# The last shared pass of a mixture-of-experts loop behind all passes of a single expert, its loads last in the queue

## The chip, the cores and the metric

The kernel runs on one core of one Trainium2 chip. The metric is the device time of one execution in microseconds (us), the median of three runs. Beside it stands one profiled execution, whose span is counted from its first to its last instruction; all rows below are from that execution.

## The reference, cut to what matters

The program is one decoder block on 256 tokens of width 1024: a convolution and an attention mixer first, then a mixture of 64 experts, of which each token takes 8. The change touches only the experts:

```
def expert_chunk(args):
    tc, cc = args                                   # 256 tokens, their weights for 64 experts
    gu = jnp.einsum('cd,edf->cef', tc, w_experts_gate_up)          # (64, 1024, 512)
    act = jax.nn.silu(gu[..., :EXPERT_DIM]) * gu[..., EXPERT_DIM:] * cc[..., None]
    return jnp.einsum('cef,efd->cd', act, w_experts_down)          # (64, 256, 1024)
...
x = x + gate2 * moe_sublayer(h, ...)      # routed experts plus one shared expert
```

An expert that no token has chosen adds nothing, so its weights need not be read.

## The kernel before

The first part of the program, up to about 379 us, computes the mixers, the router, and a table `tab` in SBUF. In the table stand two counts, `n_trio` and `n_big`, and for each window of work a start and an expert. The tokens are gathered by expert into slots, and the experts are then worked off in passes of 128 rows.

There are two kinds of pass. A single pass (`big`) works on one expert with up to 128 slots. A shared pass (`trio`) works on three experts at once, the first with 64 slots and the other two with 32 each; its matmuls take 32 columns of the array at a time. Both do the same steps: the gate and up product into `psU` (L1396 for the single pass, L1412 for the shared one), the scatter of the pass before into the accumulators (L1372, eight matmuls in two parts, in `both`), a transpose of the activation (L1381), a transpose of the selection matrix (L1386), and the down product into `psY` (L1402 or L1420). ScalarE computes the silu (L603), copies the tokens of the next pass into `hT` (L594 for a single pass, three copies at L599 for a shared one), copies `aT` (L608) and evicts the result (L612). VectorE builds the selection of the next pass (L1011) and the low half of the result (L1035).

The weights have four buffers: `BIG` for the single pass, `MID` and two `SMALL` ones for the shared pass. Each has a part for gate and up (`gu`, 2 MiB) and a part for down (`dn`, 1 MiB), and there is only one of each buffer. So a load can be issued only when the matmuls that read the old weights are through. All these loads are issued by SyncE (SP) at L317 and L321, in the order in which its program has them, onto one queue.

The order on every engine is a hardware loop over `g` from 0 to `n_trio`, with one single pass and one shared pass in each round, and a second loop for the single passes that are left. On TensorE:

```
with pe.Fori(0, n_trio) as g:
    big(g * 2, g)
    trio(g * 2 + 1, g)
with pe.Fori(n_trio, n_big) as g:
    big(g + n_trio, g)
```

In this run `n_trio` is 13 and `n_big` is 14, so that the order ends: single 12, shared 12, single 13. The first argument of `big` and `trio` is the number of the pass in the whole order, the second that of its own kind. `loop_counts` (L281) loads the two counts from the table into registers, on each of four engines. After the last pass its result is scattered (L1372 once more), multiplied by a gate, added to the residual and stored.

Of the kernel before, what the change touches and what calls it, by code (L numbers as in the profile page):

```python
# [5 lines left out]
def hybrid_conformer_fox_moe_block(  # L6
# [12 lines left out]
    fp32, fp32r, i32 = mybir.dt.float32, mybir.dt.float32r, mybir.dt.int32  # L19
    ALU = mybir.AluOpType  # L20
# [22 lines left out]
    PADDED = SLOTS + PART  # L43
    NW = 4
    CAND = 2 * E
    T_START, T_EXP = 2, 2 + CAND
    GU, DN = KD * 2 * F, KF * D
    SLOTW = GU + DN
    NBUF = 5
# [5 lines left out]
    with ctx:  # L55
        def sb(name, shape, dt=fp32):
            return ctx.enter_context(nc.sbuf_tensor(name, shape, dt))
# [44 lines left out]
        ident = sb("ident", [PART, PART])  # L102
        slotm = sb("slotm", [PART, TH, E])
        wt = sb("wt", [PART, TH, E])
        tab = sb("tab", [1, 2 + 2 * CAND], i32)
        st2 = sb("st2", [PART, 16])
        wcol = sb("wcol", [PART, 1])

# [172 lines left out]
        def loop_counts(engine):  # L281
            n_trio = engine.value_load(tab[0:1, 0:1], min_val=2, max_val=19)
            n_big = engine.value_load(tab[0:1, 1:2], min_val=3, max_val=E - 1)
            return n_trio, n_big

        def window_of(engine, j):
            return engine.value_load(tab[0:1, bass.ds(j + T_START, 1)], min_val=0, max_val=SLOTS)
# [15 lines left out]
        @block.sync  # L303
        def _(sp):
            sp.dma_start(crow, c[0].rearrange("(k p) -> k p", p=PART)).then_inc(c_in, 16)
            sp.dma_start(bada[0:PART:32, :, :], b_ada[0].rearrange("(q k n) -> q k n", q=4, k=3)).then_inc(bada_in, 16)
            sp.dma_start(xs[:, :, :], x[0].rearrange("(t p) d -> p t d", p=PART)).then_inc(x_in, 16)
            users = used_by()
            for n in range(len(pieces)):
                if n >= NBUF:  # L310
                    sp.wait_ge(*users[n - NBUF])
                    sp.wait_ge(piece_in[n % NBUF], 16 * (n // NBUF))
                sp.dma_start(piece(n), pieces[n]).then_inc(piece_in[n % NBUF], 16)  # L313


            def load_gu(b, e):
                sp.dma_start(w_gu(b), w_experts_gate_up[0, bass.ds(e, 1), :, :].rearrange(  # L317
                    "o (p k) n -> p (o k) n", p=PART)).then_inc(gu_in[b], 16)

            def load_dn(b, e):  # L320
                sp.dma_start(w_dn(b), w_experts_down[0, bass.ds(e, 1), :, :].rearrange(  # L321
                    "o (p k) n -> p (o k) n", p=PART)).then_inc(dn_in[b], 16)

            sp.wait_ge(*users[COUT])
            sp.wait_ge(*users[WOUT])
            sp.wait_ge(*users[WOUT + 1])
            sp.wait_ge(*users[SHGU])
            sp.wait_ge(*users[SHD])
            sp.wait_ge(tabs_ready, 1)
            n_trio, n_big = loop_counts(sp)  # L330
            e = expert_of(sp, 0)
            load_gu(BIG, e)
            load_dn(BIG, e)
            for s in (MID,) + SMALL:
                e = expert_of(sp, trio_rank(s, 0, n_big, n_trio))
                if s == SMALL[1]:
                    sp.wait_ge(gather_ps, 4 * KD)
                load_gu(s, e)
                load_dn(s, e)

            def load_big(g):
                e = expert_of(sp, g)
                sp.wait_ge(big_gu, g)
                load_gu(BIG, e)
                sp.wait_ge(big_dn, g)
                load_dn(BIG, e)

            with sp.Fori(1, n_trio) as g:
                load_big(g)
                es = [expert_of(sp, trio_rank(s, g, n_big, n_trio)) for s in (MID,) + SMALL]  # L350
                sp.wait_ge(trio_gu, g)
                for s, e in zip((MID,) + SMALL, es):
                    load_gu(s, e)
                sp.wait_ge(trio_dn, g)
                for s, e in zip((MID,) + SMALL, es):
                    load_dn(s, e)
            with sp.Fori(n_trio, n_big) as g:
                load_big(g)
            for t in range(TH):
                for n in range(2):  # L360
                    sp.wait_ge(fin, t * 2 + n + 1)
                    sp.dma_start(out[0, t * PART:(t + 1) * PART, n * W:(n + 1) * W],
                                 xs[:, t, n * W:(n + 1) * W]).then_inc(out_done, 16)
            sp.wait_ge(out_done, 16 * TH * 2)
# [77 lines left out]
        def _(a):  # L442
# [135 lines left out]
            a.activation(h2r[0], h2, ACT.Copy).then_inc(h2r_hi, 1)  # L578

            a.wait_ge(tabs_ready, 1)  # L580
            n_trio, n_big = loop_counts(a)

            for i in range(0, 4 * KD, 2):
                a.wait_ge(gather_ps, i + 1)
# [21 lines left out]
            def outputs(i, down, count):  # L606
                a.wait_ge(t_done, i + 1)
                a.activation(aT[:, :, :], psM[:, 0:F].rearrange("p (k n) -> p k n", k=KF), ACT.Copy).then_inc(aT_ready, 1)  # L608
                a.wait_ge(down, count)
                a.wait_ge(st_ready, i + 2)  # L610
                for n in range(2):
                    a.activation(y2[:, 0, n * W:(n + 1) * W], psY[n][:, :], ACT.Copy, scale=wcol[:, 0:1]).then_inc(y_hi, 1)  # L612

            big_input(0)
            with a.Fori(0, n_trio) as g:
                a.wait_ge(big_gu, g + 1)
                gate()
                trio_input(g)
                outputs(g * 2, big_dn, g + 1)
                a.wait_ge(trio_gu, g + 1)  # L620
                gate()
                big_input(g + 1)
                outputs(g * 2 + 1, trio_dn, g + 1)
            with a.Fori(n_trio, n_big) as g:
                a.wait_ge(big_gu, g + 1)
                gate()
                big_input(g + 1)
                outputs(g + n_trio, big_dn, g + 1)


        @block.vector
        def _(v):
# [341 lines left out]
            link(v.scalar_tensor_tensor(na, nb, 1.0, na, ALU.add, ALU.max))  # L974
            v.tensor_copy(tab[0:1, 0:1], nb)
            v.tensor_copy(tab[0:1, 1:2], na)
            v.wait_ge(tabs_ps, 1)
            v.tensor_scalar(tab[0:1, T_START:T_START + CAND], bank[0][0:1, 0:CAND], float(SLOTS), None, ALU.add)
            v.tensor_copy(tab[0:1, T_EXP:T_EXP + CAND], bank[0][0:1, CAND:2 * CAND]).then_inc(tabs_ready, 1)
# [21 lines left out]
                    v.wait_ge(gather_ps, i + 1)  # L1001
                    v.tensor_copy(hs[:, i % KD, q * W:(q + 1) * W], bank[1][:, :]).then_inc(gather_out_dve, 1)

            n_trio, n_big = loop_counts(v)
            v.wait_ge(gather_ps, 4 * KD)
            v.tensor_scalar(ST[:, :], iota[:, 0:SEQ], 0.0, None, ALU.mult).then_inc(st_ready, 1)

# [16 lines left out]
            def product(i):  # L1024
                v.wait_ge(silu_done, i + 1)
                v.tensor_tensor(act[:, :].rearrange("s (k f) -> s k f", k=KF), sg[:, :].rearrange("s (k f) -> s k f", k=KF),  # L1026
                                psU[:, F:2 * F].rearrange("s (f k) -> s k f", k=KF), ALU.mult).then_inc(act_ready, 1)
                v.wait_ge(sit_done, i + 1)
                v.tensor_scalar(ST[:, :], psU[:, 0:SEQ], 0.0, None, ALU.is_gt)  # L1029
                v.reduce_sum(wcol[:, 0:1], psU[:, 0:SEQ], AX).then_inc(st_ready, 1)  # L1030

            def outputs(i):
                for n in range(2):
                    v.wait_ge(y_hi, i * 2 + n + 1)
                    v.scalar_tensor_tensor(y2[:, 1, n * W:(n + 1) * W], psY[n][:, :], wcol[:, 0:1],  # L1035
                                           y2[:, 0, n * W:(n + 1) * W].bitcast(fp32), ALU.mult, ALU.subtract).then_inc(y_lo, 1)
# [1 line left out]
            v.tensor_scalar(y2[:, :, :], iota[:, 0:2 * D].rearrange("p (s d) -> p s d", s=2), 0.0, None,  # L1038
                            ALU.mult).then_inc(y_lo, 2)
            big_si(0)  # L1040
            with v.Fori(0, n_trio) as g:
                product(g * 2)
                trio_si(g)
                outputs(g * 2)
                product(g * 2 + 1)
                big_si(g + 1)
                outputs(g * 2 + 1)
            with v.Fori(n_trio, n_big) as g:
                product(g + n_trio)
                big_si(g + 1)  # L1050
                outputs(g + n_trio)

            v.wait_ge(all_done, 1)
            for t in range(TH):
# [8 lines left out]
        def _(pe):  # L1063
# [326 lines left out]
            def big(i, g):  # L1390
                wg, wd = w_gu(BIG), w_dn(BIG)
                pe.wait_ge(hT_ready, i + 1)
                pe.wait_ge(st_ready, i + 1)
                pe.wait_ge(gu_in[BIG], g * 16 + 16)
                for k in range(KD):
                    ins = mm(psU[:, :], hT[:, k, :], wg[:, k, :], start=(k == 0), stop=(k == KD - 1))  # L1396
                ins.then_inc(big_gu, 1)
                both(i)
                pe.wait_ge(dn_in[BIG], g * 16 + 16)
                for n in range(2):  # L1400
                    for k in range(KF):
                        ins = mm(psY[n][:, :], aT[:, k, :], wd[:, k, n * W:(n + 1) * W], start=(k == 0), stop=(k == KF - 1))  # L1402
                ins.then_inc(big_dn, 1)
# [17 lines left out]
                                     start=(k == 0), stop=(k == KF - 1))  # L1421
                ins.then_inc(trio_dn, 1)

            n_trio, n_big = loop_counts(pe)
            with pe.Fori(0, n_trio) as g:
                big(g * 2, g)
                trio(g * 2 + 1, g)
            with pe.Fori(n_trio, n_big) as g:
                big(g + n_trio, g)
            pe.wait_ge(st_ready, n_big + n_trio + 1)  # L1430
            pe.wait_ge(y_lo, n_big * 2 + n_trio * 2 + 2)
            ins = scatter(PASSES, stop=True)
# [23 lines left out]
```

## Time and profile before

| what | us |
|---|---|
| median of 3 runs | 788.98 |
| the runs | 786.12, 790.57, 788.98 |
| span of the profiled execution | 785.2 |
| TensorE busy in it | 705.0 (90%) |
| VectorE busy | 294.9 |
| ScalarE busy | 183.9 |

A separate time of the profiled execution is not recorded; its span lies 0.9 us below the fastest run and 3.75 us below the median. TensorE is busy for nine tenths of the span, but from 402 us on the DMA engines are busy without a break as well, until shortly before 760 us. What matters is which of the two is waited for at the end.

### The profile page before, as it was taken

What the parts mean: (1) busy time and instruction counts of PE and PEld (TensorE: products, weight loads), DVE (VectorE), ACT (ScalarE), POOL (GpSimd) and SP (SyncE); (2) the same over time, 40 slices, a digit from 0 to 9 for tenths busy, and PEclk for the clock granted to TensorE, in tenths of its full rate; (3) what the DMA queues carried; (4) which work ended last, traced back from release to release, by engine and by line L of the source; (5) the groups of instructions that cost most, each with busy time, mean ns of one, the idle gap of its engine ahead of it and who ended that gap; (6) DMA issues with size and microseconds to landing.
All of it is one profiled execution on the core that took longest, in us unless ns stands there. A gap on an engine that the chain in (4) does not pass through costs nothing.

```text
span 785.2 us, 9994 instructions
## 1 busy us (share of the span) xinstructions
PE 705.0 (90%) x3383; PEld 398.8 (51%) x3383; DVE 294.9 (38%) x672; ACT 183.9 (23%) x320; POOL 60.7 (8%) x50
## 2 busy tenths in 40 slices
PE   2899999797999999979899998899898998899894
PEld 1488845575787847656434343334343443334342
DVE  2233795655452425755232312312312222312314
ACT  2021432213214111312222212212212212212211
POOL 6004610404000000000000000000000000000000
PEclk9789997799999999989999999999999999999997
DMA  9998866041553100065579999999999999999961
GB/s 308 387 343 327 295 235 215 0 174 40 215 215 134 54 1 0 3 265 218 212 284 425 427 429 424 427 430 422 426 429 423 427 430 423 425 430 426 424 273 53
DMA packets 43132, 225.65 MB, mean 287 GB/s; under 512 B 3488, under 2 KB 3520, under 8 KB 29414
## 3 DMA queue, kind: packets, MB, share of 16 engines
q1 hardware_dynamic: 41528, 224.43, 71.0%
q10 hardware_dynamic: 1582, 0.94, 0.4%
q8 instruction: 13, 0.21, 0.1%
q14 instruction: 9, 0.07, 0.0%
HBM read 224.31 MB, written 1.05 MB: 287 GB/s over the span
## 4 chain that ended last, share of the span: by engine, by line
PE 56%; DMA 31%; DVE 6%; SPq 3%; issue 2%; ACT 2%; ACTq 0%; DVEq 0%
DMA raw<-n_w_experts_gate_up_dram 29%; PE bank L1129 13%; PE bank L1412 12%; PE bank L1361 4%; PE bank L1268 4%; PE bank L1229 3%; PE bank L1396 3%; DMA ring<-in_w_ada_dram 3%; PE bank L1145 2%; PE bank L1402 1%; DVE work L750 1%; PE bank L1183 1%; PE bank L1185 1%; SPq L317 1%; SPq L313 1%
## 5 line engine op out<-in xcount | busy, mean ns | idle before, releaser
L1129 PE MATMUL bank<-work,ring 128*128 128x256 f32 x512 | 119.4, 392 | 1.4 <-ACT work L476 1.4
L1412 PE MATMUL bank<-raw,hT 128*32 128x512 f32 x832 | 96.9, 619 | 21.0 <-DMA raw<-n_w_experts_gate_up_dram 21.0
L1129 PEld LDWEIGHTS bank<-work,ring 128*128 128x128 f32 x512 | 100.6, 198 | 17.3 <-issue 1.6
L1396 PE MATMUL bank<-raw,hT 128*128 128x512 f32 x224 | 101.6, 607 | 2.9 <-ACT hT L594 2.9
L1026 DVE TENSOR_TENSOR sg<-sg,bank 128x256 f32<-128x256 f32 x27 | 11.4, 421 | 171.7 <-ACT sg L603 171.7
L1412 PEld LDWEIGHTS bank<-raw,hT 128*32 128x32 f32 x832 | 30.6, 113 | 86.1 <-issue 86.1
L1396 PEld LDWEIGHTS bank<-raw,hT 128*128 128x128 f32 x224 | 42.0, 192 | 62.2 <-issue 61.3
L1372 PE MATMUL bank<-y,ST 128*128 128x512 f32 x224 | 70.8, 439 | 2.3 <-DVE y L1035 2.3
L603 ACT ACTIVATE sg<-bank 128x256 f32<-128x256 f32 x27 | 17.1, 634 | 183.8 <-PE bank L1412 100.6
L612 ACT ACTIVATE y<-bank,wcol 128x512 fp32r<-128x512 f32 x54 | 34.1, 683 | 108.4 <-PE bank L1402 54.3
L1402 PE MATMUL bank<-raw,aT 128*128 128x512 f32 x112 | 51.7, 604 | 7.3 <-ACT aT L608 7.3
L750 DVE SCALAR_TENSOR_TENSOR work<-work,convc 128x256 f32<-128x256 f32 x120 | 55.4, 530 | 0.1
L1372 PEld LDWEIGHTS bank<-y,ST 128*128 128x128 f32 x224 | 39.2, 190 | 25.8 <-issue 17.6
L1011 DVE TENSOR_SCALAR SI<-iota,slotm,wt 128x32 f32 (+2 forms) x108 | 29.2, 314 | 55.4 <-issue 55.4
L1035 DVE SCALAR_TENSOR_TENSOR y<-bank,wcol,y 128x512 fp32r<-128x512 f32 x54 | 38.0, 744 | 30.5 <-ACT y L612 30.5
L1420 PE MATMUL bank<-raw,aT 128*32 128x512 f32 x416 | 47.3, 595 | 0.0
L1402 PEld LDWEIGHTS bank<-raw,aT 128*128 128x128 f32 x112 | 20.1, 189 | 30.5 <-issue 20.1
L423 POOL TENSOR_TENSOR ring<-ring 128x2048 f32<-128x2048 f32 x4 | 24.6, 6160 | 128.4 <-ACT ring L489 128.4
L1268 PE MATMUL bank<-ring,work 128*128 128x512 f32 x64 | 27.7, 594 | 1.5 <-DVE work L853 1.5
L1229 PE MATMUL bank<-work,ring 128*128 128x256 f32 x128 | 28.3, 381 | 0.0
L1229 PEld LDWEIGHTS bank<-work,ring 128*128 128x128 f32 x128 | 24.2, 190 | 4.0 <-issue 0.8
L1029 DVE TENSOR_SCALAR ST<-bank 128x256 fp32r<-128x256 f32 x27 | 11.5, 424 | 39.1 <-PE bank L1386 39.1
(285 smaller groups left out, 692.1 us busy)
## 6 DMA issues: line engine op xcount, KB each, us to landing
raw<-n_w_experts_gate_up_dram SPq DMA_DIRECT2D x53, 2048.0 KB, 16.7
raw<-in_w_experts_down_dram SPq DMA_DIRECT2D x53, 1024.0 KB, 18.5
ring<-in_w_ada_dram SPq DMA_DIRECT2D x12, 2048.0 KB, 11.2
ring<-in_w_in_dram SPq DMA_DIRECT2D x9, 2048.0 KB, 14.2
ring<-in_w_out_dram SPq DMA_DIRECT2D x2, 2048.0 KB, 10.6
ring<-in_w_attn_out_dram SPq DMA_DIRECT2D x1, 2048.0 KB, 7.5
ring<-in_w_conv_out_dram SPq DMA_DIRECT2D x1, 2048.0 KB, 13.6
ring<-in_w_shared_gate_up_dram SPq DMA_DIRECT2D x1, 2048.0 KB, 8.3
```

The source lines that it names most:

```text
L612: a.activation(y2[:, 0, n * W:(n + 1) * W], psY[n][:, :], ACT.Copy, scale=wcol[:, 0:1]).then_inc(y_hi, 1)
L750: v.scalar_tensor_tensor(cacc[:, k, :], upad[:, k, bass.ds(j, SEQ)], convc[:, k, bass.ds(j, 1)], cacc[:, k, :], ALU.mult, ALU.add).then_in ...
L1035: v.scalar_tensor_tensor(y2[:, 1, n * W:(n + 1) * W], psY[n][:, :], wcol[:, 0:1], y2[:, 0, n * W:(n + 1) * W].bitcast(fp32), ALU.mult, ALU ...
L1129: ins = mm(b[:, kk * SEQ:(kk + 1) * SEQ], w[:, k, m * PART:(m + 1) * PART], h1T[:, k, :], start=(k == 0), stop=(k == KD - 1))
L1229: ins = mm(bank[3 + i][:, kk * SEQ:(kk + 1) * SEQ], w[:, k, m * PART:(m + 1) * PART], src[:, k, :], start=(k == 0), stop=(k == KC - 1))
L1268: ins = mm(bank[2 * t + n][:, :], gates[:, k, t * PART:(t + 1) * PART], w[:, k, :], start=(k == 0), stop=(k == KD - 1))
L1361: ins = mm(bank[i % 2][:, :], h2r[s][:, t, k * PART:(k + 1) * PART], SS[:, q % 2, t, :], start=(s == t == 0), stop=(s == 1 and t == TH - 1))
L1372: ins = mm(acc[2 * t + n][:, :], ST[:, t * PART:(t + 1) * PART], y2[:, s, n * W:(n + 1) * W], start=False, stop=(stop and s == 1))
L1396: ins = mm(psU[:, :], hT[:, k, :], wg[:, k, :], start=(k == 0), stop=(k == KD - 1))
L1402: ins = mm(psY[n][:, :], aT[:, k, :], wd[:, k, n * W:(n + 1) * W], start=(k == 0), stop=(k == KF - 1))
L1412: ins = mm(psU[c:c + 32, :], hT[:, k, c:c + 32], w_gu(s)[:, k, :], start=(k == 0), stop=(k == KD - 1))
L1420: ins = mm(psY[n][c:c + 32, :], aT[:, k, c:c + 32], w_dn(s)[:, k, n * W:(n + 1) * W], start=(k == 0), stop=(k == KF - 1))
```

## The change

The counts get two companions in the table, each one less: `last` is `n_trio - 1` and `last_big` is `n_big - 1`. `loop_counts` loads four values instead of two on each engine. The main loop runs over `last` rounds instead of `n_trio`. Behind it all single passes that are left run in one loop, and the last shared pass stands behind them, written out. On this input the order now ends: single 12, single 13, shared 12.

SP's loads follow. After the main loop it loads single 12, then the `MID` expert of the last shared pass (gate and up, then down), then the first `SMALL` expert, then single 13, and last the second `SMALL` expert. ScalarE and VectorE copy and select for the pass that now comes next, and no longer prepare a pass behind the last one.

```
 def loop_counts(engine):
     n_trio = engine.value_load(tab[0:1, 0:1], min_val=2, max_val=19)
     n_big = engine.value_load(tab[0:1, 1:2], min_val=3, max_val=E - 1)
-    return n_trio, n_big
+    last = engine.value_load(tab[0:1, T_LAST:T_LAST + 1], min_val=1, max_val=18)
+    last_big = engine.value_load(tab[0:1, T_LAST + 1:T_LAST + 2], min_val=2, max_val=E - 2)
+    return n_trio, n_big, last, last_big
...
 # SP
-with sp.Fori(1, n_trio) as g:
+with sp.Fori(1, last) as g:
     load_big(g)
     ...
-with sp.Fori(n_trio, n_big) as g:
-    load_big(g)
+load_big(last)
+sp.wait_ge(trio_gu, last)
+for s in (MID, SMALL[0], SMALL[1]):
+    if s == SMALL[1]:
+        with sp.Fori(n_trio, n_big) as g:
+            load_big(g)
+    e = expert_of(sp, trio_rank(s, last, n_big, n_trio))
+    load_gu(s, e)
+    sp.wait_ge(trio_dn, last)
+    load_dn(s, e)
...
 # ScalarE
-with a.Fori(0, n_trio) as g:
+with a.Fori(0, last) as g:
...
-with a.Fori(n_trio, n_big) as g:
+with a.Fori(last, last_big) as g:
     a.wait_ge(big_gu, g + 1)
     gate()
     big_input(g + 1)
-    outputs(g + n_trio, big_dn, g + 1)
+    outputs(g + last, big_dn, g + 1)
+a.wait_ge(big_gu, n_big)
+gate()
+trio_input(last)
+outputs(last + last_big, big_dn, n_big)
+a.wait_ge(trio_gu, n_trio)
+gate()
+outputs(last + n_big, trio_dn, n_trio)
...
 # VectorE, before the table is announced as ready
+v.tensor_scalar(tab[0:1, T_LAST:T_LAST + 1], nb, -1.0, None, ALU.add)
+v.tensor_scalar(tab[0:1, T_LAST + 1:T_LAST + 2], na, -1.0, None, ALU.add)
...
+product(last + last_big)
+trio_si(last)
+outputs(last + last_big)
+product(last + n_big)
+outputs(last + n_big)
...
 # TensorE
-with pe.Fori(0, n_trio) as g:
+with pe.Fori(0, last) as g:
     big(g * 2, g)
     trio(g * 2 + 1, g)
-with pe.Fori(n_trio, n_big) as g:
-    big(g + n_trio, g)
+with pe.Fori(last, n_big) as g:
+    big(g + last, g)
+trio(last + n_big, last)
```

Two places show what stands where. The first is SP behind the main loop. Of the names, `big_gu`, `big_dn`, `trio_gu` and `trio_dn` count the products that have read their weights, L317 or L319 is a gate and up load, and L321 or L323 a down load. Before, from the end of the main loop:

```order
L348 COMPARE_AND_BRANCH
L357 UNCONDITIONAL_BRANCH
L357 ISA
L290 TENSOR_LOAD tab
L290 ISA x2
L317 ISA [waits big_gu]
L317 DMA raw<-in_w_experts_gate_up_dram 128x4096
L321 ISA [waits big_dn]
L321 DMA raw<-in_w_experts_down_dram 128x2048
```

And now, from single 13's load on (ahead of it stand the loads of single 12, of `MID` and of the first `SMALL`):

```order
L319 ISA [waits big_gu]
L319 DMA raw<-in_w_experts_gate_up_dram 128x4096
L323 ISA [waits big_dn]
L323 DMA raw<-in_w_experts_down_dram 128x2048
L364 REGISTER_ALU
L364 COMPARE_AND_BRANCH
L292 ISA
L292 TENSOR_LOAD tab
L292 ISA x2
L319 ISA
L319 DMA raw<-in_w_experts_gate_up_dram 128x4096
L323 ISA [waits trio_dn]
```

Single 13's load was the last and now has one expert, 3 MiB, behind it.

The second place is TensorE between the gather (L1361 before) and the first single pass. Before:

```order
L282 TENSOR_LOAD tab [waits gather_out_dve,gather_out_act]
L282 ISA x2
L283 TENSOR_LOAD tab
L283 ISA x2
L1425 UNCONDITIONAL_BRANCH
L1425 ISA
L1394 ISA [waits st_ready,hT_ready]
```

And now:

```order
L282 TENSOR_LOAD tab [waits gather_out_dve,gather_out_act]
L282 ISA x2
L283 TENSOR_LOAD tab
L283 ISA x2
L284 TENSOR_LOAD tab
L284 ISA x2
L285 TENSOR_LOAD tab
L285 ISA x2
L1450 UNCONDITIONAL_BRANCH
L1450 ISA
L1419 ISA [waits st_ready,hT_ready]
```

Two table loads with two register instructions each have been added in front of the loop.

## Rows read from the trace of the kernel before

**Rows 1.** The page: chain that ended last by engine, and memory rate in 40 slices.

```profile
PE 56%; DMA 31%; DVE 6%; SPq 3%; issue 2%; ACT 2%; ACTq 0%; DVEq 0%
...
GB/s 308 387 343 327 295 235 215 0 174 40 215 215 134 54 1 0 3 265 218 212 284 425 427 429 424 427 430 422 426 429 423 427 430 423 425 430 426 424 273 53
```

**Rows 2.** The page: costliest groups; count, busy us, mean ns, idle before and releaser.

```profile
L1412 PE MATMUL bank<-raw,hT 128*32 128x512 f32 x832 | 96.9, 619 | 21.0 <-DMA raw<-n_w_experts_gate_up_dram 21.0
...
L1396 PE MATMUL bank<-raw,hT 128*128 128x512 f32 x224 | 101.6, 607 | 2.9 <-ACT hT L594 2.9
```

**Rows 3.** The page: weight loads; count, size of one, us to landing.

```profile
raw<-n_w_experts_gate_up_dram SPq DMA_DIRECT2D x53, 2048.0 KB, 16.7
raw<-in_w_experts_down_dram SPq DMA_DIRECT2D x53, 1024.0 KB, 18.5
```

**Rows 4.** Chain in order of time, last two waited landings: start, us, what.

```profile
696.77 19.36 DMA raw<-n_w_experts_gate_up_dram
...
724.58 21.08 DMA raw<-n_w_experts_gate_up_dram
```

**Rows 5.** Timeline of SP from the last main loop round: start, us, engine, line.

```profile
723.54 1.37 SPq L317 DMA_DIRECT2D raw<-n_w_experts_gate_up_dram  x3
729.67 1.36 SPq L321 DMA_DIRECT2D raw<-in_w_experts_down_dram  x3
736.72 0.33 SPq L317 DMA_DIRECT2D raw<-n_w_experts_gate_up_dram  x1
743.50 0.33 SPq L321 DMA_DIRECT2D raw<-in_w_experts_down_dram  x1
```

**Rows 6.** Windows: stretch, busy PE, PEld, DVE, ACT, POOL, PEclk, DMA share, GB/s.

```profile
723.54:745.66 22.12, 19.21 (x80) 8.75 (x79) 6.79 (x18) 6.75 (x12) 0.00 (x0) 1.00 1.00 425
745.66:760.00 14.34, 14.20 (x111) 5.72 (x112) 2.36 (x7) 2.83 (x5) 0.00 (x0) 1.00 0.91 382
```

**Rows 7.** Windows of the last three passes: single 12, single 13, shared 12.

```profile
729.41:743.33 13.92, 13.33 (x40) 6.27 (x36) 3.63 (x9) 3.65 (x7) 0.00 (x0) 1.00 1.01 428
...
758.92:772.03 13.11, 13.09 (x40) 6.25 (x36) 3.19 (x7) 3.24 (x5) 0.00 (x0) 1.00 0.01 3
745.80:758.92 13.12, 13.12 (x108) 5.09 (x108) 2.08 (x6) 1.97 (x3) 0.00 (x0) 1.00 0.98 412
```

**Rows 8.** Timeline of TensorE at the end of single 12 and behind it.

```profile
739.63 3.70 PE L1402 MATMUL bank<-raw,aT 128*128 128x512 f32 x8 [0.56 <-ACT aT L608]
745.80 7.07 PE L1412 MATMUL bank<-raw,hT 128*32 128x512 f32 x64 [2.46 <-DMA raw<-n_w_experts_gate_up_dram]
```

**Rows 9.** One line, L283 and L1425: TensorE's queue; ns min/median/max, first and last start.

```profile
L283 PEldq TENSOR_LOAD <-tab x1: 334/334/334, 378.5 to 378.5; - x1
L283 PEldq FUSED_REGOPS  x1: 151/151/151, 378.9 to 378.9; - x1
L283 PEldq SEQ_ASSERT  x1: 18/18/18, 379.1 to 379.1; - x1
...
L1425 PEldq MOVE  x1: 33/33/33, 379.2 to 379.2; - x1
```

**Rows 10.** Timeline around the first single pass: ScalarE, VectorE, TensorE.

```profile
378.12 1.06 ACT L594 ACTIVATE hT<-work 128x1024 f32 x1 [1.82 <-DVE work L1002]
378.33 0.29 DVE L1006 TENSOR_SCALAR ST<-iota 128x256 fp32r<-128x256 f32 x1 [0.87 <-issue]
...
379.59 8.82 PE L1396 MATMUL bank<-raw,hT 128*128 128x512 f32 x16 [2.86 <-ACT hT L594]
```

**Rows 11.** Chain in order of time, where the table is written.

```profile
336.60 0.13 DVE tab L976
```

**Rows 12.** TensorE after a wait at the lower clock, then a first product at the full one.

```profile
509.63 8.64 PE L1412 MATMUL bank<-raw,hT 128*32 128x512 f32 x64 [2.46 <-DMA raw<-n_w_experts_gate_up_dram]
...
729.41 7.13 PE L1396 MATMUL bank<-raw,hT 128*128 128x512 f32 x16
```

**Rows 13.** Windows, with the granted clock: after that wait, and in the first single pass.

```profile
509.40:512.82 3.42, 3.19 (x16) 0.90 (x20) 0.51 (x1) 0.00 (x0) 0.00 (x0) 0.50 1.01 419
379.70:383.11 3.41, 3.41 (x5) 1.34 (x6) 0.66 (x3) 0.00 (x0) 0.00 (x0) 0.50 1.00 428
```

More of the change, by code:

```diff
@@ L45, in hybrid_conformer_fox_moe_block @@
     CAND = 2 * E
-    T_START, T_EXP = 2, 2 + CAND
+    T_START, T_EXP, T_LAST = 2, 2 + CAND, 2 + 2 * CAND
     GU, DN = KD * 2 * F, KF * D
@@ L104, in hybrid_conformer_fox_moe_block @@
         wt = sb("wt", [PART, TH, E])
-        tab = sb("tab", [1, 2 + 2 * CAND], i32)
+        tab = sb("tab", [1, 4 + 2 * CAND], i32)
         st2 = sb("st2", [PART, 16])
@@ L329, in _ @@
             sp.wait_ge(tabs_ready, 1)
-            n_trio, n_big = loop_counts(sp)
+            n_trio, n_big, last, last_big = loop_counts(sp)
             e = expert_of(sp, 0)
@@ L580, in _ @@
             a.wait_ge(tabs_ready, 1)
-            n_trio, n_big = loop_counts(a)
+            n_trio, n_big, last, last_big = loop_counts(a)
             for i in range(0, 4 * KD, 2):
@@ L1002, in _ @@
                     v.tensor_copy(hs[:, i % KD, q * W:(q + 1) * W], bank[1][:, :]).then_inc(gather_out_dve, 1)
-            n_trio, n_big = loop_counts(v)
+            n_trio, n_big, last, last_big = loop_counts(v)
             v.wait_ge(gather_ps, 4 * KD)
@@ L1040, in _ @@
             big_si(0)
-            with v.Fori(0, n_trio) as g:
+            with v.Fori(0, last) as g:
                 product(g * 2)
@@ L1047, in _ @@
                 outputs(g * 2 + 1)
-            with v.Fori(n_trio, n_big) as g:
-                product(g + n_trio)
+            with v.Fori(last, last_big) as g:
+                product(g + last)
                 big_si(g + 1)
-                outputs(g + n_trio)
+                outputs(g + last)
+            product(last + last_big)
[3 more added lines that the diff above has]
+            outputs(last + n_big)
             v.wait_ge(all_done, 1)
@@ L1422, in trio @@
                 ins.then_inc(trio_dn, 1)
-            n_trio, n_big = loop_counts(pe)
-            with pe.Fori(0, n_trio) as g:
+            n_trio, n_big, last, last_big = loop_counts(pe)
+            with pe.Fori(0, last) as g:
                 big(g * 2, g)
                 trio(g * 2 + 1, g)
-            with pe.Fori(n_trio, n_big) as g:
-                big(g + n_trio, g)
+            with pe.Fori(last, n_big) as g:
+                big(g + last, g)
+            trio(last + n_big, last)
             pe.wait_ge(st_ready, n_big + n_trio + 1)
```

## The prediction, made before the changed kernel ran

> **What bounds the kernel now.** I read the page first. The chain that ended last is 56% TensorE and 31% DMA, and the memory rate stands at 422 to 430 GB/s from the 22nd slice on, about 412 us, and falls in the 39th [rows 1]. So the expert loop is bound by loads. The costliest groups say where this is felt: the 832 matmuls of L1412 are 13 shared passes of 64, and all their idle time, 21.0 us, was ended by a gate and up load; the 224 of L1396 are 14 single passes of 16, which waited for no load worth the name [rows 2]. Each round therefore waits once, ahead of its shared pass.
>
> The chain in order of time gives the period. The last two awaited loads landed at 696.77 + 19.36 = 716.13 and 724.58 + 21.08 = 745.66 us, 29.53 us apart [rows 4]. A round loads four experts of 3 MiB [rows 3], 12.58 MB, which at 29.53 us is 426 GB/s; the window up to 745.66 shows 425 [rows 6]. Hence 2 MiB (2.10 MB) take 4.92 us of the queue, and 1 MiB 2.46 us.
>
> The tail is another thing. After 745.66 us TensorE waits for no load: shared 12 takes 13.12 us and single 13 takes 13.11, back to back, up to 772.03 [rows 7], and then come the result, the scatter and the store, 13.2 us to the end. The loads are all in by about 759: the window from 745.66 to 760.00 moved 382 x 14.34 = 5.5 MB [rows 6]. So two things set the end: the moment when the second last pass can start, and from then on the work of TensorE alone. The last load is not waited for at all.
>
> **The change part by part.** The change ranks passes and loads by the last load. I ask instead when the last but one pass can start, and how TensorE goes on from there.
>
> 1. *Order of loads.* Before, shared 12 could start when its three gate and up loads had landed. Ahead of these in the queue, counted from the end of shared 11's loads, stood single 12 (3 MiB) and these three (6 MiB), 9 MiB. Now the last but one pass is single 13. Ahead of its gate and up load stand single 12 (3), `MID` (3), the first `SMALL` (3), and itself (2), 11 MiB. That is 2 MiB or 4.92 us later: 750.6 instead of 745.66 us on the old clock. Behind this TensorE has two passes of 13 us each, so the last shared pass can't start before 763.7, while its last load lands by the same count at about 758, as single 13's did before. The last load is again not waited for, and the delay goes straight to the end: **+4.9**. The queue must not run dry for this to hold. SP issued at 723.54, 729.67, 736.72 and 743.50 [rows 5], and its new waits (`trio_gu`, `trio_dn`, `big_gu`, `big_dn`) are for the same products at the same times, so `MID` goes out at about 723.5, its down part and the first `SMALL` behind 729.7, single 13 at 736.7, and the second `SMALL` behind 743. After 723.54 us 425 x 22.12 = 9.4 MB and then 5.5 MB moved [rows 6], 14.9 in all, of which 12.6 were issued after it; so 2.3 MB or 5.4 us of work stood in the queue at that moment. In the new order `MID`'s 2 MiB make this last until 733.9, and each later load goes out 4 us or more before the queue would be empty, so I cost this at nothing. The lower bound of the term: the landing of a load is when the slowest DMA engine is through. At 745.66 0.8 MB of what was issued behind had moved already (6.3 MB were to come, 5.5 moved), 1.9 us. If single 13's load lands without such a lag, the term is 3.0. The two cases have the same kind of load behind them, so I take 4.9.
>
> 2. *Two more table loads on each engine.* The table is written by single-element instructions on VectorE that lie on the chain; L976 took 0.13 us, and it follows its forerunner after 0.07 [rows 11]. Two more make +0.13. On ScalarE and SP the loads stand where both wait for others anyway (the gather's products, for which SP holds its fourth expert back as well), nothing. On TensorE they stand between the gather and the first single pass. The load of L283 started at 378.5 and, with its two register instructions, ended at 379.1; the loop's entry is at 379.2 [rows 9], and the first matmul started at 379.59, 0.41 us after `hT` was ready at 379.18 [rows 10]. ScalarE is named as the releaser, but TensorE's own queue was later. So each further load costs its whole step, 378.5 to 379.2, some 0.65 us: **+1.3**. VectorE writes `ST`, which the first pass also waits for, at 378.33 + 0.29 = 378.62, and two more loads put this at about 379.8, ahead of TensorE's 380.9. This shift is not caught up later: the queue was empty between the first rounds (212 and 284 GB/s in the 20th and 21st slice [rows 1]), the loads of round 1 wait for TensorE's products, and only from about 412 us on is the queue never empty. Bounds: 0 if the 0.41 us has another cause and the loads hide behind `hT`, 1.5 at most. The Trainium skill, page "DMA: Bandwidth & Descriptors", section "Latency and other measured facts", gives about 600 ns as the floor of such a load; the rows show 334 ns for the load and 0.65 us for the step; by the page's figure alone the term would be 1.2.
>
> 3. *Single 13 is now followed by a shared pass.* Where that is so, ScalarE makes three copies instead of one ahead of `aT`, and TensorE waits 0.56 us in front of L1402 [rows 8]. Single 12, which had a shared pass behind it, took 13.92 us, and single 13, which had not, 13.11 [rows 7]. After the change it is single 13 that takes 13.92: **+0.8**. Single 12 becomes shorter by as much, which only lengthens the wait behind it. The last shared pass has nothing to prepare; but shared 12 waited for neither engine before [rows 7], so this gives nothing back.
>
> 4. *The clock.* TensorE waited 2.46 us ahead of shared 12 and kept the full clock of 2.4 GHz; L1412 took 7.07 us [rows 8]. After the same wait at 507.17 us the granted clock was 0.50, that is 1.2 GHz, from 509.40 to 512.82 [rows 13], and the same 64 matmuls took 8.64, 1.57 more [rows 12]. The first single pass came behind 2.86 us without matmuls, ran at 0.50 until 383.11 [rows 13], and its sixteen took 8.82 [rows 10] against 7.13 [rows 12]: 1.69 more. The new wait ahead of single 13 is 750.6 minus the end of single 12 at about 742.5, 8 us, more than twice as long as either, so I expect the fall, and single 13 stands where every us counts. The nearest row is the single pass: **+1.7**. Bounds: 0 if the clock holds through the wait, as it did behind 2.46 us once, and 3.4, twice the row, if the lower clock lasts twice as long. The Trainium skill, page "TensorE: Matmul & The Clock Gate", section "Part 1: The HAM clock gate", says that the clock drops when the array idles and comes back only after sustained work, and that the penalty varies between runs; by that rule too the fall is expected here, and the sum stays as it is.
>
> The sum is 4.9 + 0.13 + 1.3 + 0.8 + 1.7 = 8.8 us. The span goes from 785.2 to 794.0. The median lies 3.75 above the span of the profile, and I carry this over: 788.98 + 8.8 = **797.8 us**, 1.1% slower.
>
> **The rivals.**
>
> *The clock holds, or the table loads hide.* Then 1.7 or 1.3 or both are missing: 5.8 to 7.5 us, 794.8 to 796.5. For it: the same wait left the clock alone at 745.80. Against: the length of the new wait, and the 0.41 us.
>
> *Single 13's load does not wait its turn (the other side, not slower).* It is issued at 736.7, when `MID` and the first `SMALL` still stand in the queue. If the DMA engines served all issued loads side by side, its 2 MiB could land by about 746, as early as the load that was waited for before. Then term 1 is gone, the wait is 3 us and term 4 may go too; what stays is 0.13 + 1.3 + 0.8 = 2.2 us, 791.2, within 0.5%. It decides from a landing before 747. And if the last shared pass could start as its last load lands, at 758, 5.7 us earlier than I count, the end would be earlier by about 1 us than before without the other terms; even this is no gain of 0.5%. Against it: the awaited landings at 29.53 us intervals fit the bytes ahead of them in order, and a load takes 16.7 us to land in the middle of the field [rows 3] where its own bytes need 4.9, so that it spends the rest behind others. The Trainium skill, page "DMA: Bandwidth & Descriptors", section "Queues, rings and completion order", says that each DMA engine takes its descriptors in ring order but that completion is not strictly first in, first out for the issuing engine; by this small overtakings are possible, not one of 2 MiB.
>
> *The queue runs dry (slower still).* SP now waits for `trio_dn` and `big_dn` between the loads of the last shared pass. If the second `SMALL` load went out late enough to land behind the end of single 13, over 5.7 us later than I count, the last pass would wait. At that point the term grows one for one; a gap of 8 us would make it 800. The issue times [rows 5] speak against it.
>
> **How the numbers follow.** The forecast, all four terms about as sized, 0.68. A smaller slowdown by the first rival 0.16. Not slower by the second 0.08. Slower still by the third 0.05. Something unseen that gains 0.03. The lower bounds are 3.0 + 0.13 + 0 + 0.8 + 0 = 3.9, so 792.9; the upper 4.9 + 0.13 + 1.4 + 0.8 + 3.4 = 10.6, so 799.6. The runs before spread over 4.5 us, so I widen by a us or two: 792.5 to 801.5. A change of 0.5%, 3.9 us, is about what a measurement of this kernel can tell from none. Slower by more than that: 0.68 + 0.16 + 0.05, of which I take 0.01 off for a sum at the very low end, 0.88. Same 0.10. Faster 0.02.
>
> **What would show it.** In the profile after, TensorE starts the first single pass about 1.3 us later after the gather. At the end there is one idle stretch of about 8 us ahead of the last L1421 (L1396 before), ended by a gate and up load, with the granted clock at 0.50 behind it, and its sixteen matmuls take some 8.8 us. Then L1437 (L1412 before) starts without waiting for a load. The memory rate stays above 420 GB/s until 13 us behind the old landing. I am wrong if single 13 starts within 3 us of the end of single 12, if the last L1437 waits for a load, or if the rate has a hole after 723 us.

## The result, and the profile after

The changed kernel takes 797.16 us in the median of four runs (796.19 to 797.28), the kernel before 788.50 (786.12 to 790.57, with one run more than above). The ratio is 1.0122 with a 95% interval of 1.0096 to 1.0149: slower by 1.2%. (The two medians alone lie 8.7 us or 1.1% apart, which is inside that interval.) The forecast was 797.8 and slower.

The page of the changed kernel answers to [rows 1, 2]. First its chain and rate, then the two groups of gate and up products (single passes are now L1421, shared ones L1437):

```profile
span 795.4 us, 9997 instructions
...
PE 57%; DMA 30%; DVE 6%; SPq 2%; issue 2%; ACT 2%; ACTq 1%; DVEq 0%
...
L1421 PE MATMUL bank<-raw,hT 128*128 128x512 f32 x224 | 105.4, 625 | 12.3 <-DMA raw<-n_w_experts_gate_up_dram 8.2
L1437 PE MATMUL bank<-raw,hT 128*32 128x512 f32 x832 | 96.8, 619 | 18.4 <-DMA raw<-n_w_experts_gate_up_dram 18.4
```

The shared passes lost one wait (18.4 us of waits for loads against 21.0), and the single ones got a new one of 8.2 us. They also became busier by 3.8 us, with the same 224 matmuls. That is work at a lower clock. The chain in order of time shows the last two landings that were waited for, as [rows 4] did (start, us, what):

```profile
696.12 21.08 DMA raw<-n_w_experts_gate_up_dram
...
737.78 13.92 DMA raw<-n_w_experts_gate_up_dram
```

They are at 717.20 and 751.70 us, 34.50 apart, where before it was 29.53. The timeline of TensorE shows the head and the end of the loop (start, us, engine, line, count, idle before and its releaser), to be held against [rows 8, 10, 12]:

```profile
379.76 9.86 PE L1421 MATMUL bank<-raw,hT 128*128 128x512 f32 x16 [4.13 <-DVE ST L1026]
...
730.47 7.13 PE L1421 MATMUL bank<-raw,hT 128*128 128x512 f32 x16
...
739.97 3.60 PE L1427 MATMUL bank<-raw,aT 128*128 128x512 f32 x8
751.75 9.90 PE L1421 MATMUL bank<-raw,hT 128*128 128x512 f32 x16 [8.18 <-DMA raw<-n_w_experts_gate_up_dram]
...
764.75 3.70 PE L1427 MATMUL bank<-raw,aT 128*128 128x512 f32 x8 [0.55 <-ACT aT L619]
768.38 7.07 PE L1437 MATMUL bank<-raw,hT 128*32 128x512 f32 x64
...
783.92 3.18 PE L1397 MATMUL bank<-y,ST 128*128 128x512 f32 x8 [2.33 <-DVE y L1055]
```

Single 12 is over at 743.57. Single 13 then waits 8.18 us for its load and needs 9.90 us for sixteen matmuls that took 7.13 one pass earlier. Shared 12 follows at 768.38 and waits for no load. Windows of the same stretches, with the columns of [rows 6]:

```profile
743.57:751.75 8.18, 0.00 (x1) 0.00 (x1) 1.41 (x2) 1.26 (x2) 0.00 (x0) 0.72 1.01 426
747.00:751.75 4.75, 0.00 (x1) 0.00 (x1) 0.00 (x0) 0.00 (x0) 0.00 (x0) 0.51 0.98 414
751.75:757.40 5.65, 5.65 (x7) 2.50 (x8) 0.00 (x0) 0.00 (x0) 0.00 (x0) 0.50 1.01 426
```

The queue had no hole while TensorE waited (414 to 426 GB/s), and the granted clock fell to 0.50, 1.2 GHz, during the wait and stayed there for the first 5.6 us of the work behind it.

SP's issues, against [rows 5]:

```profile
725.26 0.33 SPq L319 DMA_DIRECT2D raw<-n_w_experts_gate_up_dram  x1
730.74 0.33 SPq L323 DMA_DIRECT2D raw<-in_w_experts_down_dram  x1
732.02 0.33 SPq L319 DMA_DIRECT2D raw<-n_w_experts_gate_up_dram  x1
732.54 0.33 SPq L323 DMA_DIRECT2D raw<-in_w_experts_down_dram  x1
737.78 0.33 SPq L319 DMA_DIRECT2D raw<-n_w_experts_gate_up_dram  x1
```

The last of these is single 13's gate and up load. It was issued at 737.78 and landed 13.92 us later, behind everything that was queued ahead of it.

### The profile page after: what moved, and what is told of

Read it like the earlier page. It is cut to its first block, busy times and chain, and to the rows that moved or that the text cites. A ratio compares the mean times of both kernels' runs of the same rounds, so it can differ in the third digit from the quotient of the medians.

```text
span 795.4 us, 9997 instructions
## 1 busy us (share of the span) xinstructions
PE 708.9 (89%) x3383; PEld 400.0 (50%) x3383; DVE 295.4 (37%) x672; ACT 182.9 (23%) x319; POOL 61.2 (8%) x50
## 4 chain that ended last, share of the span: by engine, by line
PE 57%; DMA 30%; DVE 6%; SPq 2%; issue 2%; ACT 2%; ACTq 1%; DVEq 0%
DMA raw<-n_w_experts_gate_up_dram 27%; PE bank L1154 13%; PE bank L1437 12%; PE bank L1386 4%; PE bank L1421 4%; PE bank L1293 3%; PE bank L1254 3%; DMA ring<-in_w_ada_dram 3%; PE bank L1170 2%; PE bank L1427 1%; PE bank L1445 1%; DVE work L768 1%; PE bank L1208 1%; PE bank L1210 1%; PE bank L1397 1%
## 5 line engine op out<-in xcount | busy, mean ns | idle before, releaser
L1421 PE MATMUL bank<-raw,hT 128*128 128x512 f32 x224 | 105.4, 625 | 12.3 <-DMA raw<-n_w_experts_gate_up_dram 8.2
L1437 PE MATMUL bank<-raw,hT 128*32 128x512 f32 x832 | 96.8, 619 | 18.4 <-DMA raw<-n_w_experts_gate_up_dram 18.4
L1421 PEld LDWEIGHTS bank<-raw,hT 128*128 128x128 f32 x224 | 43.5, 200 | 73.9 <-issue 64.0
L1437 PEld LDWEIGHTS bank<-raw,hT 128*32 128x32 f32 x832 | 30.3, 113 | 83.6 <-issue 83.6
## 6 DMA issues: line engine op xcount, KB each, us to landing
ring<-in_w_in_dram SPq DMA_DIRECT2D x9, 2048.0 KB, 13.9
```

The source lines that it names most:

```text
L1437: ins = mm(psU[c:c + 32, :], hT[:, k, c:c + 32], w_gu(s)[:, k, :], start=(k == 0), stop=(k == KD - 1))
```

## The experiments

Two theories stood against each other. Mine: the place of single 13's load in the queue sets when the last but one pass starts, and the rest of the loss comes from table loads on TensorE's path and from the clock. The rival is the idea that the change rests on: the place of the last load decides the end. All kernels of a group of runs shared runs of the kernel before on the same chip; those medians were 787.12 for the first four, 786.65 for the next four and 785.38 for the last. Each group ran on a chip of its own, so between groups, and with the changed kernel, I compare ratios and stretches of traces rather than medians. "Ratio" is always the time against the kernel before.

### The table loads alone

The kernel before with the two table entries and the two loads per engine, in the old order.

```
 n_big = engine.value_load(tab[0:1, 1:2], min_val=3, max_val=E - 1)
+engine.value_load(tab[0:1, T_LAST:T_LAST + 1], min_val=1, max_val=18)
+engine.value_load(tab[0:1, T_LAST + 1:T_LAST + 2], min_val=2, max_val=E - 2)
 return n_trio, n_big
```

> The kernel before with the two added table entries and the two added table loads on each engine, and nothing of the new order. My theory (term 2 of the sum): the loads stand on TensorE's own path between the gather and the first single pass, 0.65 us each, and the table entries cost 0.13 us, so 1.4 us more than before, a ratio of 1.0018, with the gap between the last gather matmul and the first single pass 1.3 us longer. Rival: they hide behind the copy of hT, ratio 1.000 and the gap as before. If more than 3 us of the surplus of 8.7 us appear here, the order is not the main cause.

Measured: 790.26 us, ratio 1.0044 (1.0021 to 1.0067), that is 3.5 us with an interval of 1.7 to 5.3. TensorE's first single pass (columns as above):

```profile
379.00 9.86 PE L1400 MATMUL bank<-raw,hT 128*128 128x512 f32 x16 [4.14 <-issue]
```

The gap behind the gather is 4.14 us instead of 2.86, so 1.28 longer, as expected. The rival that they hide is out. But the sixteen matmuls took 9.86 us too, where [rows 10] had 8.82: 1.04 us more. I had not counted this. The loads cost 1.3 us of waiting and 1.0 us of slower work behind it.

The expectation had also said that more than 3 us here would make the order not the main cause, and the measured 3.5 is just above that. The trace shows what else is in it. From the end of the gather to the start of shared 12 this kernel needs 371.39 us (746.25 - 374.86) and the one before 369.07 (745.80 - 376.73). That is 2.32 more, the two parts above and nothing else. Behind it two stretches were slower whose waits are those of before:

```profile
746.25 8.77 PE L1416 MATMUL bank<-raw,hT 128*32 128x512 f32 x64 [2.46 <-DMA raw<-n_w_experts_gate_up_dram]
...
776.49 3.32 PE L1376 MATMUL bank<-y,ST 128*128 128x512 f32 x8 [2.30 <-DVE y L1039]
```

Shared 12's product took 1.70 us more than in [rows 8], at a granted clock of 0.51 from 746.25 to 749.70, and the last scatter 0.68 more than the 2.64 of before. That the table loads cause these two is not shown. The next run settles the question of the order, since it has the new order without the added loads.

### The new order with two table loads

The table holds the two counts less one in place of the counts, and nothing else is added to it.

```
-n_trio = engine.value_load(tab[0:1, 0:1], min_val=2, max_val=19)
-n_big = engine.value_load(tab[0:1, 1:2], min_val=3, max_val=E - 1)
-last = engine.value_load(tab[0:1, T_LAST:T_LAST + 1], min_val=1, max_val=18)
-last_big = engine.value_load(tab[0:1, T_LAST + 1:T_LAST + 2], min_val=2, max_val=E - 2)
-return n_trio, n_big, last, last_big
+last = engine.value_load(tab[0:1, 0:1], min_val=1, max_val=18)
+last_big = engine.value_load(tab[0:1, 1:2], min_val=2, max_val=E - 2)
+return last + 1, last_big + 1, last, last_big
```

> The changed kernel, but the table holds the two counts less one instead of all four, and each engine loads two values and adds one in its registers. The order of passes and loads is the new one. My theory: 1.4 us less than the changed kernel, about 795.8 us, ratio to before 1.009 to 1.010. Rival (the loads hide): as the changed kernel, 797.2.

Measured: 794.79 us, ratio 1.0093 (1.0066 to 1.0121), against 1.0122 of the changed kernel. So 7.3 us of the slowdown stand without any added load, and the order is the main cause. The two ratios are 2.3 us apart, though their intervals overlap. The traces are sharper:

```profile
377.77 8.83 PE L1417 MATMUL bank<-raw,hT 128*128 128x512 f32 x16 [2.80 <-ACT hT L603]
...
727.83 7.13 PE L1417 MATMUL bank<-raw,hT 128*128 128x512 f32 x16
...
749.08 9.28 PE L1417 MATMUL bank<-raw,hT 128*128 128x512 f32 x16 [8.14 <-DMA raw<-n_w_experts_gate_up_dram]
```

Gap and first product are those of before again. All six traced kernels with four loads have a gap of 4.1 us there, and the product behind it takes 9.9 to 10.1 us. The three with two loads in that place and nothing put into the gap have 2.8 to 2.9 and 8.8 us. The wait ahead of single 13 is untouched by this, 8.14 us: it belongs to the order.

### TensorE kept busy through the wait

```
-with pe.Fori(last, n_big) as g:
+big(last + last, last)
+for j in range(17):                       # 9 in the second run
+    mm(psM[:, :], ident[:, :], hs[:, 0, 0:W], start=True, stop=True)
+with pe.Fori(n_trio, n_big) as g:
     big(g + last, g)
```

> The changed kernel with 17 more matmuls of 128x512 into a free bank of PSUM behind single 12, about 7.3 us of TensorE work whose result nobody reads, in the wait for single 13's load. My theory (term 4): the granted clock stays at 1.00, the sixteen matmuls of single 13's gate and up product take 7.1 us instead of 9.9, and the span is 2.8 us shorter than that of the changed kernel, 792.6; single 13 starts at the same time or up to 0.3 us later. Rival (the longer product has another cause, such as the weight loads still in flight, or the clock falls anyway): 9.9 us as before and a span of 795.4.

Measured: 803.98 us, ratio 1.0210 (1.0175 to 1.0245), span 799.1. The span missed my 792.6, because I had sized the added work wrongly: an fp32 matmul shows as two records of 0.43 us, and 17 of them are 34.

```profile
743.89 14.75 PE L1455 MATMUL bank<-work,ident 128*128 128x512 f32 x34
758.48 7.03 PE L1421 MATMUL bank<-raw,hT 128*128 128x512 f32 x16
```

The load was issued at 738.26 and landed 13.9 us later, at 752.2, and the added matmuls ended 6.4 us after that. The other half of the expectation came out: behind them the product took 7.03 us. The run was made again with nine.

> As the run with the added matmuls behind single 12, with 9 of them instead of 17: the 17 showed as 34 records of 0.43 us, 14.75 us of work in a wait of 8.2, and so ended 6.7 us after the load had landed. Nine are 7.7 us. My theory: single 13 starts where it does in the changed kernel, at about 751.8 on its clock, its sixteen matmuls take 7.1 us instead of 9.9 as in the run with 17, and the span is 2.8 us below that of the changed kernel, 792.6; median about 794.5. Rival (the added matmuls delay single 13 or the clock falls anyway): 795 or more.

Measured: 794.32 us, ratio 1.0096 (1.0073 to 1.0119), span 792.4.

```profile
742.76 7.89 PE L1455 MATMUL bank<-work,ident 128*128 128x512 f32 x18
751.10 7.13 PE L1421 MATMUL bank<-raw,hT 128*128 128x512 f32 x16 [0.45 <-DMA raw<-n_w_experts_gate_up_dram]
```

Single 13 starts 21.29 us behind the start of single 12, as in the changed kernel (21.28), and its product is back at 7.13 us. The span is 3.0 us shorter for doing more work: 2.77 from the product and 0.66 from an earlier start of single 12, less 0.47 in a slower last scatter. (The ratios agree in direction, but their intervals overlap.) So term 4 is shown by the traces: 2.8 us of the loss are the clock.

### Two MiB fewer, three MiB more ahead of single 13

Fewer: the down loads of `MID` and of the first small expert behind single 13's loads. More: the second small expert ahead of them.

```
 # fewer
 load_gu(MID, es[0])
 load_gu(SMALL[0], es[1])
 with sp.Fori(n_trio, n_big) as g:
     load_big(g)
 sp.wait_ge(trio_dn, last)
+load_dn(MID, es[0])
+load_dn(SMALL[0], es[1])
 load_gu(SMALL[1], es[2])
 load_dn(SMALL[1], es[2])
 # more: all three experts first, then
+with sp.Fori(n_trio, n_big) as g:
+    load_big(g)
```

> The changed kernel with the two down loads of MID and of the first small expert, 1 MiB each, moved from ahead of single 13's loads to behind them; nothing else. My theory (term 1 is linear in the MiB that stand ahead of single 13's gate and up load, 2.46 us each): that load lands 4.9 us earlier, single 13 starts at about 746.8 instead of 751.75 and waits 3.3 us instead of 8.2, and the span is 790.5 if its product still takes 9.9 us, 787.7 if the clock holds. Rival (the last load's place decides): the end stays at 795, since the last load lands as late as before.

> The changed kernel with the second small expert's 3 MiB ahead of single 13's loads too, so that these are the last in the queue again, with the order of passes left as changed. My theory: 3 MiB more ahead are 7.4 us more, single 13 starts at about 759.1, and the span is about 802.8. Rival (the last load's place decides): the last loads, now single 13's, land where the last ones did before, and the end moves by no more than 2 us.

Measured: 792.60 us, ratio 1.0074 (1.0048 to 1.0100), and 806.21 us, ratio 1.0233 (1.0205 to 1.0261). Single 12 and single 13 in the first, then in the second:

```profile
732.36 7.13 PE L1423 MATMUL bank<-raw,hT 128*128 128x512 f32 x16
...
748.64 8.83 PE L1423 MATMUL bank<-raw,hT 128*128 128x512 f32 x16 [3.17 <-DMA raw<-n_w_experts_gate_up_dram]
```

```profile
732.17 7.13 PE L1420 MATMUL bank<-raw,hT 128*128 128x512 f32 x16
...
760.82 9.60 PE L1420 MATMUL bank<-raw,hT 128*128 128x512 f32 x16 [15.53 <-DMA raw<-n_w_experts_gate_up_dram]
```

The executions are shifted against each other by their first halves, so I count from the start of single 12 to the start of the last but one pass. The MiB are those that must land between shared 11's loads and that start:

| kernel | MiB | us |
|---|---|---|
| before (shared 12 is last but one) | 9 | 16.39 |
| two MiB fewer | 9 | 16.28 |
| changed | 11 | 21.28 |
| three MiB more | 14 | 28.65 |

From 9 to 11 MiB (the second row and the third) that is 2.50 us per MiB, and from 11 to 14 it is 2.46: a line. The rival wanted the end to stay: it moved by 3.8 us down and 9.0 us up in the spans (791.6 and 804.4 against 795.4), although the same bytes were loaded. The first half was 1.9 and 1.7 us later in these two than in the changed kernel. Counted from the start of single 12 to the end of the span the moves are 5.7 down and 7.3 up (59.24 and 72.23 us against 64.93). Of these 5.0 and 7.4 are the landing, and the rest is the clock: single 13's product took 8.83 and 9.60 us against 9.90, the last scatter 3.58 and 3.44 against 3.18.

### The new order with the buffers exchanged

The order of passes stays that of the changed kernel, and the two table loads are those of the second run above, so the neighbour to compare with is that run (794.79 us). Single 13 goes into the second small buffer, which is free once shared 11 is through, and the third expert of shared 12 into the big one once single 12 has read it.

```
-load_big(last)
+with sp.Fori(last, last_big) as g:
+    load_big(g)
+e = expert_of(sp, last_big)
 sp.wait_ge(trio_gu, last)
...
+load_gu(SMALL[1], e)
+sp.wait_ge(trio_dn, last)
+load_dn(SMALL[1], e)
+es = [expert_of(sp, trio_rank(s, last, n_big, n_trio)) for s in (MID,) + SMALL]
+load_gu(MID, es[0])
+load_gu(SMALL[0], es[1])
+sp.wait_ge(big_gu, last_big)
+load_gu(BIG, es[2])
+load_dn(MID, es[0])
+load_dn(SMALL[0], es[1])
+sp.wait_ge(big_dn, last_big)
+load_dn(BIG, es[2])
...
+big(last + last_big, last, SMALL[1])
+trio(last + n_big, last, (BIG, last_big))
```

> The new order of passes, with two table loads, and the buffers of the last two passes exchanged: single 13 is loaded into the second small buffer, right behind single 12, and the third expert of the last shared pass into the big buffer once single 12 has read it; the three down loads of the last shared pass come last. Single 13's gate and up load has 3 MiB ahead of it instead of 9. My theory (term 1, the place of single 13's load in the queue is what costs): TensorE waits for no load behind single 12, single 13 starts at about 742.3, shared 12 at about 756.2, and the span is about 783.3, 2 us below the kernel before and 12 below the changed one; ratio to before 0.997. Rival (the place of the last load decides, as the change assumes): the last loads land as late as in the changed kernel, so the end stays within 2 us of 795.

Measured: 784.85 us, ratio 0.9964 (0.9945 to 0.9983), span 782.0. It is faster than both kernels.

```profile
737.28 3.60 PE L1429 MATMUL bank<-raw,aT 128*128 128x512 f32 x8
740.72 7.03 PE L1423 MATMUL bank<-raw,hT 128*128 128x512 f32 x16
...
754.50 7.07 PE L1441 MATMUL bank<-raw,hT 128*32 128x512 f32 x64
...
770.04 3.48 PE L1399 MATMUL bank<-y,ST 128*128 128x512 f32 x8 [2.33 <-DVE y L1057]
```

No wait for a load is left behind single 12, and the last three passes run back to back. So the order of passes itself was not at fault; the load that had to stand so far back for want of a buffer was. The gain over the kernel before is that one wait: from the start of single 12 to the start of the last scatter the traces show 42.27 us here (770.04 - 727.77) and 44.92 before (774.33 - 729.41), 2.65 less, of which 2.46 is what TensorE waited ahead of shared 12 [rows 8].

### Two finer points on top of it

Loading TensorE's two values earlier, in its wait ahead of the gather:

```
 select(0)
+n_trio, n_big, last, last_big = loop_counts(pe)
 for q in range(4):
```

> The version with exchanged buffers, in which TensorE also loads its two table values earlier, in its wait for VectorE ahead of the gather, instead of between the gather and the first single pass. My theory: the first single pass then starts as soon as hT is ready, 0.4 us earlier, and may meet the clock a little higher: a span of 781 to 781.6 against 782.0, ratio to before 0.996. Rival: the 0.41 us have another cause, and the span stays at 782.0.

Measured: 784.43 us, ratio 0.9975 (0.9959 to 0.9990), span 782.9. The gap went from 2.84 to 2.58 us, so the loads had stood in the way by 0.26, not 0.41. The first product took 8.82 us as before. The span missed the expected 781 to 781.6, in an execution whose gather ended 2.2 us later than that of the run before; in the time the 0.26 us can't be seen.

Two matmuls more behind the gather and two behind the last shared pass, instead:

```
+keep_warm(2)          # mm(psM[:, :], ident[:, :], iota[:, 0:W]), result not read
 pe.wait_ge(gather_out_act, 2 * KD)
...
 trio(last + n_big, last, (BIG, last_big))
+keep_warm(2)
```

> The version with exchanged buffers, with two matmuls of 128x512 added behind the gather and two behind the last shared pass, whose results nobody reads, so that TensorE's waits of 2.8 and 2.3 us there shrink to about 1.1 and 0.6. My theory (a wait of TensorE is paid a second time by the lower clock of the work behind it, as the first single pass took 8.8 to 9.9 us against 7.1 and the last scatter 3.5 against 2.7): the first product takes 7.1 us instead of 8.8, the last scatter 2.7 instead of 3.5, and the span is 2 to 2.5 us below 782.0, ratio to before about 0.993 to 0.994. Rival (the clock at these places is set by earlier work, or the added matmuls come too late): a span of 782 and a ratio of 0.996 to 0.9975.

Measured: 781.93 us, ratio 0.9949 (0.9925 to 0.9973), span 778.9. TensorE at both places:

```profile
374.70 1.88 PE L1393 MATMUL bank<-iota,ident 128*128 128x512 f32 x4
377.70 7.13 PE L1428 MATMUL bank<-raw,hT 128*128 128x512 f32 x16 [1.12 <-ACT hT L609]
...
765.91 1.98 PE L1393 MATMUL bank<-iota,ident 128*128 128x512 f32 x4
768.31 2.11 PE L1404 MATMUL bank<-y,ST 128*128 128x512 f32 x8 [0.42 <-DVE y L1057]
```

The first product took 7.13 us instead of 8.82 and the last scatter 2.11 instead of 3.48, 3.1 us together, which is the difference of the spans (the two executions reach the first product within 0.07 us of each other). Of this only the 1.7 us of the first product are firm, since all four traces with a gap of 2.6 to 2.9 us show 8.8 there. The last scatter took 2.76 us in the run before this one, without any added matmul. With its median this kernel is the fastest of all here, though its interval overlaps that of the one without the added matmuls.

## Why the prediction was right

Direction, size and mechanism held. Term by term, in us, from the two traces:

| term | forecast | measured |
|---|---|---|
| 1, single 13's load 2 MiB later | 4.9 | 4.97 (34.50 - 29.53) |
| 2, table entries | 0.13 | 0.13 (VectorE's stretch from the second entry to the instruction behind the entries: 335.41 to 335.60, before 336.60 to 336.66) |
| 2, table loads on TensorE | 1.3 | 1.27 (4.13 - 2.86) |
| 3, shared pass behind single 13 | 0.8 | 0.75 (single 13 took 16.63, less the 2.77 of the clock, against 13.11 [rows 7]) |
| 4, clock behind the wait | 1.7 | 2.8 (9.90 - 7.13) |
| not in the sum: clock in the first single pass | 0 | 1.04 (9.86 - 8.82) |
| not in the sum: clock in the last scatter | 0 | 0.54 (3.18 - 2.64, before's scatter at 774.33); with no matmuls added ahead of it, it took 2.6 to 3.7 in the traces, so this may be chance |

Term 1 is the step that carried the forecast, and it is shown by four kernels on one line. The queue served its loads in order, so the second rival is out: single 13's load was issued at 737.78, landed 13.92 us later and did not overtake. The third is out as well, since the queue moved 423 GB/s from 724.60 to the landing, the lowest of the windows of several us was 414, and shared 12 waited for nothing. (I had named 420 GB/s as the mark; the 4.75 us at 414 fall short of it, the whole wait at 426 does not.) The lower bound of term 1, a landing without the lag of the slowest engine, did not occur.

Term 4 was right in kind and too small. I took the row of a wait of 2.86 us for one of 8 us; the clock fell during the wait, and then stayed low for 5.6 us of work instead of 3.4. The bound of 3.4 us held it. The sign that the sixteen matmuls take some 8.8 us did not come out; they took 9.90. Term 2 was short in the same way: I counted the wait and not what a longer wait does to the clock of the first pass, 1.0 us. This is the step that was missing, and the run with the table loads alone shows it. (A slip without weight: the text bounds the table loads by 1.5 us, the upper sum takes 1.4.)

So the terms came to 11.3 us rather than 8.8: from the end of the gather to the end of the span it is 419.77 us against 408.47. The gather happened to end 1.1 us earlier in the profiled execution, which gives the 10.2 between the spans (795.4 - 785.2). The medians moved by 8.7 only. The reason is in how I went from span to time. I carried over 3.75 us between the span of before and its median. The profiled execution of the changed kernel has a time of its own, 797.21, which is 1.8 above its span, and for the others it is 1.6 to 1.8 too. So the execution of before that was profiled was a quick one, some 1.5 us below its median of 788.50, and I added 3.75 + 8.8 where 1.8 + 10.2 would have been right. That the forecast stands 0.6 us from the median is thus partly luck; with 11.3 for the terms the ratio's interval, 7.6 to 11.7 us, would still have held it. One thing that makes an execution of before quick or slow shows in the run with the table loads alone: behind the same wait of 2.46 us its shared 12 took 1.70 us longer, because the clock fell, where the profiled one of before kept it. Whether this is what separates that execution from its median is not shown.

## What to carry to other kernels

When a stage is bound by loads and its tail by one engine, ask what the last but one piece of work waits for, not the last: count the bytes ahead of each awaited load, and the engine's work behind it. An order of work that looks better may only be so if the buffers let its loads stand early enough. And a wait of TensorE on the critical path may be paid a second time in the clock of the work behind it: here 1.6 to 2.9 us behind waits of 2.5 to 15.5 us, though a wait of 2.46 us sometimes cost nothing. A few matmuls into a free bank can win that back, if they end before the awaited load lands.

## What the runs showed of the hardware that I had not expected

The length of a wait shows in the work behind it, not only in itself: behind 2.6 to 3.2 us without matmuls the sixteen matmuls of a single pass took 8.8 us, behind 4.1 us 9.9 to 10.1, behind 8.2 us 9.3 and 9.9, behind 15.5 us 9.6, and behind added work, with at most 1.1 us of waiting left, 7.0 to 7.1. It did not grow further with waits of 8 or 15 us. And it is not a function of the wait alone: 2.46 us left the clock at full speed once and not another time [rows 8, 12], and the same shared 12 took 7.07 us behind 2.46 us in the kernel before and 8.77 behind 2.46 us with the table loads alone. The Trainium skill, page "TensorE: Matmul & The Clock Gate", section "Part 1: The HAM clock gate", says that the penalty varies with when the work begins, and the 9.3 and 9.9 us behind nearly the same wait (8.14 and 8.18) agree with that.
